# Layer B's keys and values turned by VectorE, DRAM and ScalarE instead of TensorE

## The reference

```
q, k, v = split(silu(conv(proj)));  q = l2norm(q) * SCALE;  k = l2norm(k)
lmat = where(strict, (kb @ k.T) * decay, 0)                 # per chunk and head, kb = k * beta
u, w = triangular_solve(I + lmat, [v * beta, kb * exp(gc)])
aqk = (q @ k.T) * decay;  kdec = k * exp(g_last - gc)
step:  v_new = u - w @ S;  o = qg @ S + aqk @ v_new;  S = S * exp(g_last) + kdec.T @ v_new
```

## Time and profile before

| | |
|---|---|
| time, median of 3 | 2109.37 us (2108.5 to 2114.82) |
| the profiled execution | 2113.68 us, span 2111.6 us |
| TensorE busy | 2072.5 us, 98% of the span |
| VectorE, ScalarE, GpSimd busy | 997.2, 697.7, 454.6 us |
| mean granted TensorE clock | 0.993 of full |

### The profile page before, as it was taken

How to read it: one execution, slowest core, us unless ns; L and a number is a source line. 1 busy time by engine, 2 the same in 40 slices (tenths; PEclk the granted TensorE clock), 3 DMA queues, 4 the chain that set the end, 5 groups by cost and what they waited for, 6 DMA issues and landing times. The chain is left out here.

```text
span 2111.6 us, 36594 instructions
## 1 busy us (share of the span) xinstructions
PE 2072.5 (98%) x14446; PEld 1487.2 (70%) x14446; DVE 997.2 (47%) x2664; ACT 697.7 (33%) x1631; POOL 454.6 (22%) x639
## 2 busy tenths in 40 slices
PE   8999999999999999999999999999999999999998
PEld 6888888888888887555466777767666666665444
DVE  5234354354435345331238777777876133332252
ACT  4121321322131122231135555555564344532101
POOL 0522232222223213300023134322331200020000
PEclk9999999999999999999999999999998999999999
DMA  7411301211131127668412122222210461134451
GB/s 235 161 43 41 107 27 51 80 41 43 41 97 37 50 83 223 237 202 255 131 31 74 73 95 83 93 87 82 73 48 13 137 256 31 41 105 134 134 161 50
DMA packets 210238, 210.34 MB, mean 100 GB/s; under 512 B 14261, under 2 KB 181653, under 8 KB 209150
## 3 DMA queue, kind: packets, MB, share of 16 engines
q1 hardware_dynamic: 198070, 148.27, 23.7%
q0 software_dynamic: 12000, 59.73, 7.4%
HBM read 179.56 MB, written 68.23 MB: 117 GB/s over the span
## 5 line engine op out<-in xcount | busy, mean ns | idle before, releaser
L887 PE MATMUL bank<-arena 128*128 128x256 f32 (+1 forms) x2688 | 631.7, 386 | 0.0
L887 PEld LDWEIGHTS bank<-arena 128*128 128x128 f32 x2688 | 494.5, 190 | 75.3
L2104 PE MATMUL bank<-arena 128*128 128x352 f32 x1296 | 452.5, 470 | 0.1
L2104 PEld LDWEIGHTS bank<-arena 128*128 128x128 f32 x1296 | 220.8, 191 | 71.4 <-issue 1.0
L2909 PE MATMUL bank<-arena 128*128 128x352 f32 x576 | 176.4, 459 | 0.0
L3399 PE MATMUL bank<-arena 128*128 128x512 f32 x360 | 167.5, 599 | 0.0
L2162 PEld LDWEIGHTS bank<-arena 128*128 128x128 f32 x864 | 129.9, 194 | 45.7 <-DVE arena L2646 3.7
L2909 PEld LDWEIGHTS bank<-arena 128*128 128x128 f32 x576 | 106.6, 190 | 53.3
L1341 POOL TENSOR_TENSOR arena<-arena 128x272 f32<-128x272 f32 (+1 forms) x48 | 31.5, 656 | 507.4 <-ACT arena L1061 487.4
L2162 PE MATMUL bank<-arena 128*128 128x128 f32 x864 | 135.0, 280 | 1.5 <-DVE arena L2646 1.0
L1323 POOL TENSOR_TENSOR arena<-arena 128x512 f32<-128x512 f32 x96 | 122.8, 1279 | 11.3 <-POOL arena L1323 0.9
(11 more groups left out here) (432 smaller groups left out, 2754.1 us busy)
## 6 DMA issues: line engine op xcount, KB each, us to landing
arena<-in_w_in_a SPq DMA_DIRECT2D x48, 512.0 KB, 5.2
arena<-in_w_in_b SPq DMA_DIRECT2D x40, 512.0 KB, 7.5
arena<-in_cache_win_k SPq DMA_DIRECT2D x48, 256.0 KB, 6.1
arena<-in_cache_win_v SPq DMA_DIRECT2D x48, 256.0 KB, 4.7
out<-arena SPq DMA_DIRECT2D x40, 256.0 KB, 3.4
arena<-in_w_mem_kv SPq DMA_DIRECT2D x16, 512.0 KB, 8.1
arena<-in_cache_mem_k SPq DMA_DIRECT2D x32, 256.0 KB, 4.3
arena<-in_cache_mem_v SPq DMA_DIRECT2D x32, 256.0 KB, 4.2
```

Of the source, the lines that this page charges most:

```text
L887: m = nc.tensor.matmul(o[:, 0:hi - lo], w, y, start=k == 0 and i in (0, 1, 3, 5), stop=k == KH - 1, skip_group_check=i in (2, 4, 6))
L2104: m = nc.tensor.matmul(bank[j % 3][:, 0:PART], ring.slots[:, (B1 + b) % RING, k, :], part_in(k, part_), start=k == 0, stop=k == KD - 1)
```

## The change

Steps "kt" and "vt" are gone. In slots 6 and 7 of group G, VectorE turns keys and values of group G + 1 with two stream transposes (`kv_turned`), which turn each 32x32 block in place, into a buffer of 128x1024 words. For group 0 this is done ahead of the first slot. SP sends the buffer to DRAM in one transfer (`turned_away`) and takes it back in four, which put the blocks where a full transpose has them (`turned_back`). In slots 8 to 11 of group G (5 to 8 of group 15) ScalarE scales one chunk of keys and one of values in each slot (`scale_turned`). The landing place is the buffer of the gate pieces, so in group 15 the projection units move from the first slots to the last. The semaphores of `Chain` now come from the pool that is freed between phases.

```diff
-    PREP = {5: ("ra",), 7: ("kt",), 8: ("kk",), 9: ("qk",), 15: ("vt",)}
+    PREP = {5: ("ra",), 8: ("kk",), 9: ("qk",)}
+    AT_TURN = {6: 0, 7: 1}
+    scale_at = lambda G: 5 if G == 2 * HB - 1 else 8
-    slots += [[(0, 1)] * 16, [(0, 2)] * 4 + [(0, 1)] * 12]
+    slots += [[(0, 1)] * 16, [(0, 0)] + [(0, 1)] * 10 + [(0, 2)] * 5]
...
+        def turned_away(g):
+            sp.wait_ge(turnd, 2 * (g + 1))
+            sp.dma_start(turned_kept[g % 2], turned_in[g]).then_inc(kv_away, 16)
+        def turned_back(g):
+            sp.wait_ge(kv_away, 16 * (g + 1))
+            after(sp, kvs, 4 * g)
+            src = turned_kept[g % 2].rearrange("(a y) (b m) -> b y a m", a=4, b=4)
+            for b in range(4):
+                sp.dma_start(kv_words[quarter(b)].rearrange("p (a m) -> p a m", a=4), src[b]).then_inc(kv_in, 16)
...
+        for G in range(NG_):
+            if G % 2 and G < NG_ - 1:
+                weights(3 * (G // 2) + 8)
+                weights(3 * (G // 2) + 9)
+            if G + 1 < NG_:
+                turned_away(G + 1)
+                turned_back(G + 1)
+            if G % 2 == 0:
+                weights(3 * (G // 2) + 7)
...
+            if i == 1 and part_ == 0:
+                act.wait_ge(kvs, 4 * NG_)
...
+        def scale_turned(g, cl):
+            w, c = hd[:, g // 2 % 2], GR[g % 2][0] + cl
+            if not cl:
+                act.wait_ge(kv_in, 64 * (g + 1))
+                act.wait_ge(hdv, 3 * g + 3)
+                if g > 1:
+                    left(act, g - 2, f"su{GR[g % 2][1] - 1}")
+            wide = lambda v: v.rearrange("p (a x) -> p a x", x=32)
+            nc.scalar.activation(wide(kdec[:, c, :]), kv_back[:, :, 0, cl, :], ACT.Copy, scale=w[:, KD_, c:c + 1])
+            nc.scalar.activation(wide(vb[:, c, :]), kv_back[:, :, 1, cl, :], ACT.Copy,
+                                 scale=w[:, KN, c:c + 1]).then_inc(kvs, 1)
...
-            elif name == "kt":
-                dve.wait_ge(hdv, 3 * G + 3)
-                nc.vector.tensor_tensor(kdec[:, cs, :], bk(b), factors_of[:, KD_, cs].unsqueeze(2)
-                                        .to_broadcast([P, 4, P]), ALU.mult).then_inc(rd_dve, 1)
-            elif name == "vt":
-                nc.vector.tensor_tensor(vb[:, cs, :], bk(b), factors_of[:, KN, cs].unsqueeze(2)
-                                        .to_broadcast([P, 4, P]), ALU.mult).then_inc(rd_dve, 1)
...
+        def kv_turned(G, i):
+            h, gr = G // 2, G % 2
+            dve.wait_ge(sild, 3 * G + 2 + i)
+            if G and not i:
+                dve.wait_ge(kv_away, 16 * G)
...
+            x = qkvT[:, h % 2, 1 + i, gr * 512:(gr + 1) * 512].rearrange("p (c b x) -> p c b x", c=4, b=4)
+            nc.vector.transpose(turned_kv[G][:, :, i].rearrange("p b c x -> p c b x"), x).then_inc(turnd, 1)
...
         turned(0, "kk")
         turned(0, "qk")
+        kv_turned(0, 0)
+        kv_turned(0, 1)
         for w in range(CW):
             conv(1, 2, w)
```

More of the change, by code:

```diff
@@ L525, in _ @@
     def _(dve):
-        own = Chain(nc, dve, "in_dve")
+        own = Chain(sem, dve, "in_dve")
         def norm(n):
@@ L1130, in _ @@
     def _(dve):
-        own = Chain(nc, dve, "dve_a")
+        own = Chain(sem, dve, "dve_a")
         def evacuate(t, i):
@@ L1300, in _ @@
     def _(pool):
-        own = Chain(nc, pool, "pool_a")
+        own = Chain(sem, pool, "pool_a")
         def weight_sums(pair, ns):
@@ L1747, in _ @@
     def _(dve):
-        own = Chain(nc, dve, "wa_dve")
+        own = Chain(sem, dve, "wa_dve")
         def add(n, half):
@@ L1930, in build @@
     vb = mv[:, 0:2, :].rearrange("p a b -> p (a b)").rearrange("p (c e) -> p c e", e=P)
+    turned_in = [brT[:, HB - 2, 0:1024]] * (2 * HB - 1) + [xpad[:, 0, 0:1024]]
+    turned_kv = [w.rearrange("p (b i c x) -> p b i c x", b=4, i=2, c=4) for w in turned_in]
+    kv_words = sb[:, ZM[0]:ZM[0] + 1024]
+    kv_back = kv_words.rearrange("p (a i c x) -> p a i c x", a=4, i=2, c=4)
     flat = lambda v: v.rearrange("p a b -> p (a b)")
@@ L2078, in state_away, with weights @@
             sp.dma_start(p_delta[0, 0, h], S_of(h, NT)).then_inc(s_out, 16)
-        for b in range(3 * HB):
+        def turned_away(g):
[7 more added lines that the diff above has]
+                sp.dma_start(kv_words[quarter(b)].rearrange("p (a m) -> p a m", a=4), src[b]).then_inc(kv_in, 16)
+        def weights(b):
             if b % 3 == 2 and b // 3 >= 3:
@@ L2082, in _ @@
             ring.load(sp, B1 + b + 1)
-        state_away(HB - 3)
-        ring.load(sp, B2 + RING)
+        for b in range(7):
+            weights(b)
+        turned_away(0)
+        turned_back(0)
+        for G in range(NG_):
[7 more added lines that the diff above has]
+                weights(3 * (G // 2) + 7)
         state_away(HB - 2)
@@ L2208, in chunk_step @@
                 readout(pe, g, f"zt{LEVELS - 1}")
-                readout(pe, g, f"ks{c}" if c else "vt")
+                if c:
+                    readout(pe, g, f"ks{c}")
+                else:
+                    pe.wait_ge(kvs, 4 * g + 1)
                 to(g, f"tr{c}", [(MT[:, c, :], r_sb[:, c % 2, :] if c else vb[:, c, :])])
@@ L2227, in turned @@
                 to(G, "qk", [(ch(k_, c), ch(q, c)) for c in cs])
-            elif name == "kt":
-                to(G, "kt", [(ch(k_, c), None) for c in cs])
-            elif name == "vt":
-                to(G, "vt", [(ch(v, c), None) for c in cs])
         def matrix_step(G, s):
@@ L2475, in _ @@
                     out_roots(NG_ - 1)
+                if G < NG_ and 0 <= s - scale_at(G) < 4:
+                    scale_turned(G, s - scale_at(G))
                 for u in ended(units_at(G, s)):
@@ L2489, in _ @@
     def _(dve):
-        own = Chain(nc, dve, "b_dve")
+        own = Chain(sem, dve, "b_dve")
         stepped = [0]
@@ L2746, in _ @@
                     chunk_step(G - 1, s)
+                if s in AT_TURN and G + 1 < NG_:
+                    kv_turned(G + 1, AT_TURN[s])
                 if s == AT_INV:
@@ L2772, in _ @@
     def _(pool):
-        own = Chain(nc, pool, "b_pool")
+        own = Chain(sem, pool, "b_pool")
         def prefix(h, i):
@@ L3009, in _ @@
     def _(dve):
-        own = Chain(nc, dve, "m_dve")
+        own = Chain(sem, dve, "m_dve")
         def conv_turned(t):
@@ L3487, in _ @@
     def _(act):
-        own = Chain(nc, act, "d_act_own")
+        own = Chain(sem, act, "d_act_own")
         def squared(o):
@@ L3558, in _ @@
     def _(dve):
-        own = Chain(nc, dve, "wb_dve")
+        own = Chain(sem, dve, "wb_dve")
         gt2 = lambda v: v[:, 64:66].unsqueeze(2)
```

20 lines of the change are left out of this document (13 added, 7 removed).

## The result

Measured side by side, the kernel before took 2111.76 us and the changed kernel 2254.73 us (medians of four runs each): ratio 1.0677, 95% interval 1.0653 to 1.0700. The change made the kernel 143 us slower where 7.6 us less were forecast.

A forecast was written before the change was run, and what follows sets the result against it. TensorE's own instruction list was taken to bound layer B's steady part. Groups 2 to 12 gain 8.8 us; 8.8 - 0.7 + 0.9 + 0.7 - 2.1 = 7.6 faster, so 2101.8 us, own range 2100 to 2103.5, with rivals 2095 to 2110.

The forecast's parts named there:

- What is added on DMA: Round trip of keys and values through DRAM each group: 4 to 8 us against 27.6 us of room.
- weight loads stay hidden: SP's queue: weight blocks are asked for some 20 slots before use, so loads behind the round trip cost nothing.
- fifth rival: Late return by a slow strided DMA, 74 us, stretching each group by 46 us to some 2800; chance 0.01.
- group 0: Prologue transposes on VectorE delay group 0's first block matmul: 1.16 us lost, vt gives 0.44, together -0.7.
- Steady group: Groups 2 to 12: vt saves 0.44 us and kt 0.36 each, about 33.3 instead of 34.07 us; 8.8 in all.
- VectorE's transpose: Two 128x512 transposes in slots 6 and 7, 0.71 us each (between 0.58 and 1.24), costing nothing.
- ScalarE's pair: Two scalings in each of slots 8 to 11: 0.64 us a pair, 41 us in all, costing nothing.
- Groups 13 to 15: Layer B's end: groups 13 and 14 together gain 0.7 us; group 15, with projection units moved, loses 2.1.
- kt gives nothing: Group 13: VectorE sets the pace, so removing kt saves nothing there, while vt saves 0.6 us.
- first rival: Another clock fall from TensorE's waits in group 15: some 5 us lost, 2107 us; chance 0.2.
- Rivals 2 and 3: All 32 removed sets count, 14.1 us, 2095.3, chance 0.1; or half the steady gain is lost, 2106, chance 0.12.
- Rival 4: ScalarE becomes the chain in slots 8 to 11: at 3 us a pair, 2118 us; decides from about 2.3; chance 0.1.

The follow-up runs named there:

- e9: The changed kernel with each early cache copy split in two transfers, each meant to lie on four DMA engines: 2132.53 us.
- e1: The changed kernel without GpSimd's 12 early cache copies, so part of the outputs is left out: 2104.65 us.
- e4: The complete changed kernel with the cache copies written as 16 pieces outermost, spread over 16 DMA engines: 2104.86 us.
- e7: The changed kernel with the key and value round trip issued from ScalarE's DMA queue, away in slot 8, back in slot 13: 2289.93 us.
- e8: The changed kernel with cache copies on 16 engines, and group 0's two VectorE transposes moved behind the prologue convolution: 2103.49 us.
- e12: The changed kernel with the round trip issued from ScalarE's queue and the cache copies spread over 16 engines: 2112.95 us.
- e3: The kernel before with its cache copies cut in 8 KB runs, which were joined again: 2112.52 us.
- e5: The kernel before without TensorE's 32 transpose sets in layer B, using unturned keys and values, no round trip: 2103.21 us.
- e11: The changed kernel with cache copies on 16 engines, and each of ScalarE's eight scalings a group done three times: 2190.77 us.
- e10: The changed kernel with each early cache copy on two DMA engines as before, but in 4 KB pieces: 2261.23 us.

## Why the prediction was wrong, point by point

- **The step that failed is "What is added on DMA".** It gave the round trip 4 to 8 us against 27.6 us of room. The transfer away took 22.4 us in the median and up to 37.4, the way back up to 39.8, and what counts is the sum of both ways against 36 us (e9). The mechanism missing from it is contention on two DMA engines, held by the long packets of the GpSimd queue's cache copies; shown by e1 (copies gone: 2.7 us median) and e4 (copies spread: 3.3 us median, and 8.9 us less time than before). Its sentence that weight loads stay hidden was right for TensorE and wrong for the queue: nobody waits for the weights, but the round trip stands behind them in the queue and lands some 10 us later for it (e7).
- **The fifth rival** named a late return, at 1 in 100, for another reason (a slow strided DMA). That reason is refuted: alone, the return takes 2.5 us.
- **With the contention removed every other term can be read in e4.** Difference to before at the first block matmul of a group (L2178, here L2214), in us of layer B:

```
place        forecast   e4
group 0        +1.2    +0.4
group 12       -8.5    -9.2
group 13       -9.0    -9.6
group 14       -9.7   -10.1
group 15      -11.4   -11.2
layer's end    -7.5    -7.2
```

Forecast values are the running sum of the prediction's terms; e4's come from the starts of these matmuls and the layer's two marks (group 12: 1526.37 - 1102.84 against 1536.84 - 1104.16). e4 took 2104.86 us against 2113.71, 8.9 less. In the profiled executions, 8.5 apart, 7.2 are layer B's and 1.3 the shift of the layer's start, which isn't the change's. That the layer's end comes so near the forecast is in part luck: up to group 14 e4 is 0.4 to 0.8 us ahead of it, and group 15 takes this back, within the 1.5 us by which this place varies.

- **Steady group:** 33.28 us ((1526.37 - 1193.56) / 10) against the 33.3 forecast. The distance behind VectorE's turn is the 0.06 us that was taken. In e4, one of the groups:

```profile
1259.70 0.31 DVE L2696 STREAM_TRANSPOSE arena<-arena 128x128 f32<-128x128 f32 x1
...
1260.07 0.44 PE L2214 MATMUL bank<-arena 32*32 32x16 f32 x32
```

- **VectorE's transpose** 128x512 takes 0.70 us (median of 32), where the line between the bounds gave 0.71. **ScalarE's pair** takes 0.68 us instead of 0.64, and ScalarE's busy time grows by 36 us where 41 were forecast.
- **Group 0:** the loss was 0.4 us, not 1.2, because 0.65 us of hidden waiting were filled (e8).
- **Groups 13 to 15:** TensorE waits 1.15, 0.49 and 1.04 us ahead of the block matmul. The first is the 0.71 of before and the 0.44 of the removed set, as forecast ("kt gives nothing"). In group 15 the four waits are 0.74, 0.30, 1.04 and 1.19 us where the prediction had 0.7, 0.5, 0.25 and 1.1. The lower clock comes once in e4, as before (0.66 in 1570 to 1590 us); the second fall of the first rival did not come there. It did come in e12 and in e3, which has nothing of the change, for 3.4 us at 1610 us each, so it isn't the change's. What is owed after group 15's slot 7 is 4.0 us where 3.8 were worked out.
- **Rivals 2 and 3** (all sets count: 14.1; half of the gain): neither; e5 gives 9.0 us in layer B.
- **Rival 4** was never tested by the change itself, whose pair takes 0.68 us; e11 shows its price to be about six times what I wrote.

What stays open: where GpSimd's issue limit in e10 lies, and how a late landing divides exactly between its own packets and the weights ahead of them, since in the changed kernel the copy's end came first and let both through.

## What to carry to other kernels

Before a transfer is put on the path, read the maximum and not the median of what its queue's transfers take in that stretch, and then name every long transfer in flight beside it: how many packets at a time and how long each says how many DMA engines it holds and for how long. A background copy that harms nobody while all loads are asked for 20 slots ahead becomes the bound once a round trip needs every engine within one group; write it with 16 pieces outermost, strided so that they aren't joined again, and do this with such a change and not instead of it. Idle time of an engine with a dependent list is not room: ask for each gap who waits on the next instruction.

## What the runs showed of the hardware

- A DRAM-to-DRAM copy of 2 MB written as two rows ran as packets of 65,024 bytes at 2.40 us each, two at a time, and landed after 41.5 us (median); with 16 pieces outermost the same bytes landed in 8.9.
- On a held engine a 512-byte packet of another queue, 0.027 us long, passed at one per 2.4 us packet. A transfer of 512 KB in 128 packets, alone 2.6 us, took 26.5 us (median) beside such a copy and up to 37.4 with two weight blocks ahead of it.
- Adjacent runs in a transfer's pattern are joined before packets are made: 8 KB runs came out as 65,024 bytes.
- The same copies as pieces of 4 KB added 119,000 packets of 4 bytes to GpSimd's queue (138,464 packets in all against 12,000) and held GpSimd up to 43.4 us at an issue.
- In the group with TensorE's waits of 4.81 and 13.68 us the granted clock was 0.82, and TensorE was busy 4.5 us longer.
